# The first up projection fed row block by row block, later transfers held back, and two transposes moved into the third unit

## The reference

```python
def rmsnorm(x, g):
    y = x * lax.rsqrt(jnp.mean(x * x, axis=-1, keepdims=True) + EPS)
    return y * g

def swiglu(x, w_gate, w_up, w_down):
    return (jax.nn.silu(x @ w_gate) * (x @ w_up)) @ w_down

x = x + 0.5 * swiglu(rmsnorm(x, ffn1_norm), ffn1_w_gate, ffn1_w_up, ffn1_w_down)
# then: a mixer (gated delta rule and spatial gating), two more feed-forwards with a
# norm between them, a Mamba-2 mixer with a short convolution, cross attention,
# a fourth feed-forward and a final norm
```

## Time and profile before

| | us |
|---|---|
| time, median of 3 runs | 1371.12 (1370.67 to 1371.12) |
| the profiled execution's own time | 1371.11 |
| its span, first to last instruction | 1369.3 |
| TensorE busy | 1356.1 |
| ScalarE busy | 706.9 |
| VectorE busy | 622.0 |
| GpSimd busy | 548.8 |
| mean granted TensorE clock | 0.999 of full |

### The profile page before, as it was taken

One profiled execution on the slowest core, in us unless ns is written; L12 is line 12 of the kernel. 1 busy time (PEld: TensorE's weight loads), 2 busy tenths in 40 slices (PEclk: granted clock), 3 DMA queues, 4 the chain that ended last, 5 costly groups with the idle time before them and its releaser, 6 DMA issues.

```text
span 1369.3 us, 16611 instructions
## 1 busy us (share of the span) xinstructions
PE 1356.1 (99%) x6542; PEld 1130.5 (83%) x6542; DVE 622.0 (45%) x746; ACT 706.9 (52%) x910; POOL 548.8 (40%) x190
## 2 busy tenths in 40 slices
PE   8999999999999999999999999999999999999997
PEld 6888888998888888888888888888888888888886
DVE  4333346864333343333336559764335632433334
ACT  6444447345544445444347787657434644544432
POOL 2444443453544444444543331034535522444443
PEclk9999999999999999999999999999999999999999
DMA  9655554223555455555554555345754442655550
GB/s 362 217 184 184 185 184 154 93 90 127 200 184 184 169 176 211 197 187 189 188 192 154 217 176 193 123 154 174 289 182 169 178 176 96 217 195 184 184 184 31
DMA packets 38369, 244.21 MB, mean 178 GB/s; under 512 B 5888, under 2 KB 6304, under 8 KB 10272
## 3 DMA queue, kind: packets, MB, share of 16 engines
q1 hardware_dynamic: 35968, 234.66, 49.3%
q10 hardware_dynamic: 2336, 8.65, 1.7%
HBM read 242.21 MB, written 1.08 MB: 178 GB/s over the span
## 4 chain that ended last, share of the span: by engine, by line
PE 95%; DVE 2%; SPq 1%; ACT 1%; DMA 1%; issue 0%; POOL 0%; ACTq 0%; DVEq 0%
PE acc L329 27%; PE acc L331 27%; PE acc L330 27%; PE work L930 2%; PE acc L2468 2%; PE work L527 1%; PE work L845 1%; PE acc L2469 1%; SPq L499 1%; PE work L1752 1%; PE work L369 1%; DVE conv_out L879 1%; DMA raw<-in_t_ffn_up 1%; PE work L2492 1%; PE work L2515 1%; DVE wlo L310 0%
## 5 line engine op out<-in xcount | busy, mean ns | idle before, releaser
L310 POOL TENSOR_TENSOR wlo<-raw,whi 128x2048 fp32r<-128x2048 f32 (+1 forms) x105 | 488.2, 4653 | 642.2 <-ACT whi L305 634.3
L305 ACT ACTIVATE whi<-raw 128x2048 fp32r<-128x2048 f32 x222 | 415.8, 1884 | 93.6 <-PE acc L331 87.3
L329 PE MATMUL acc<-whi,xT 128*128 128x512 f32 x1120 | 448.0, 400 | 3.1 <-DVE xT L296 2.8
L331 PE MATMUL acc<-whi,xT 128*128 128x512 f32 x1120 | 437.8, 391 | 0.0
L330 PE MATMUL acc<-wlo,xT 128*128 128x512 f32 x1120 | 436.7, 390 | 0.0
L310 DVE TENSOR_TENSOR wlo<-raw,whi 128x2048 fp32r<-128x2048 f32 x117 | 301.6, 2578 | 239.4 <-ACT whi L305 239.2
L329 PEld LDWEIGHTS acc<-whi,xT 128*128 128x128 f32 x1120 | 210.7, 188 | 47.2 <-issue 2.7
L331 PEld LDWEIGHTS acc<-whi,xT 128*128 128x128 f32 x1120 | 210.4, 188 | 45.0
L330 PEld LDWEIGHTS acc<-wlo,xT 128*128 128x128 f32 x1120 | 211.0, 188 | 40.4 <-issue 0.2
L329 PE MATMUL acc<-whi,hid_hi 128*128 128x512 f32 x352 | 137.8, 391 | 0.0
L331 PE MATMUL acc<-whi,hid_lo 128*128 128x512 f32 x352 | 137.2, 390 | 0.0
(11 more groups left out here) (381 smaller groups left out, 1382.1 us busy)
## 6 DMA issues: line engine op xcount, KB each, us to landing
raw<-in_t_ffn_up SPq DMA_DIRECT2D x86, 1024.0 KB, 5.0
raw<-in_t_m_in SPq DMA_DIRECT2D x52, 1024.0 KB, 5.1
raw<-in_t_ffn_down SPq DMA_DIRECT2D x40, 1024.0 KB, 4.9
raw<-in_t_m_os SPq DMA_DIRECT2D x8, 1024.0 KB, 7.0
raw<-in_t_ffn_down SPq DMA_DIRECT2D x8, 512.0 KB, 3.3
raw<-in_t_m_out SPq DMA_DIRECT2D x4, 1024.0 KB, 5.1
sum_rows<-row_scratch ACTq DMA_DIRECT2D x4, 1024.0 KB, 4.7
raw<-in_t_m_oa SPq DMA_DIRECT2D x4, 1024.0 KB, 5.1
```

Of the source, the lines that this page charges most:

```text
L305: act.activation(granule(whi, u, i), granule(raw, u, i), ACT.Copy).then_inc(hi_ready, 1)
L310: eng.tensor_tensor(granule(wlo, u, i), granule(raw, u, i), granule(whi, u, i).bitcast(F32), ALU.subtract).then_inc(lo_odd if g % 2 else l ...
L329: pe.matmul(to, xhi[:, kt, tok], hi, start=first, stop=False)
L331: return pe.matmul(to, xlo[:, kt, tok], hi, start=False, stop=last)
```

## The change

- Unit 0's weights come in single row blocks for granule 0, x pieces 0 and 1 singly. ScalarE rounds one row block of weights and one x piece in turn for all eight, VectorE makes all eight low parts (GpSimd had the last two).
- TensorE orders each row block of unit 0 as two hi-hi products (both token tiles), two hi-lo, two lo-hi, with a wait of its own ahead of each pair.
- Granule 2 is transferred, rounded and made low in two halves. Granule 3's low part moves from GpSimd to VectorE.
- SyncE waits for an earlier landing before each next group of transfers; the 16 parameter transfers move behind the up units' loads.
- In the first layer the transposes of hidden chunk 0 move from the middle of unit 1 to the middle of unit 2, ahead of those of chunk 1.
- Granule 4's transfer waits for `lo_even` at 5, which is the first half of granule 2's low part (`FIRST_LO` has 4 in place of 3; granule 0 counts four).

```diff
-FIRST_HI, FIRST_LO, FIRST_XLO = 4, (3, 1), 6
+FIRST_HI, FIRST_LO, FIRST_XLO = 7, (4, 3), 6
...
     def multiply_first(pe, u, banks):
...
+            pe.wait_ge(hi_ready, kt + 1)
+            pe.wait_ge(xhi_done, kt + 1)
+            for t in range(NT):
+                pe.matmul(banks[t], xT_hi[:, kt, toks[t]], hi[:, j, :], start=kt == 0, stop=False)
+            pe.wait_ge(lo_odd if i else lo_even, j + 1)
+            for t in range(NT):
+                pe.matmul(banks[t], xT_hi[:, kt, toks[t]], lo[:, j, :], start=False, stop=False)
             pe.wait_ge(xlo_done, kt + 1)
             for t in range(NT):
-                mm = triple(pe, banks[t], xT_hi, xT_lo, kt, t, hi[:, j, :], lo[:, j, :], kt == 0, kt == KD - 1)
+                mm = pe.matmul(banks[t], xT_lo[:, kt, toks[t]], hi[:, j, :], start=False, stop=kt == KD - 1)
...
         if f == 0:
-            load_first(sp, 0, (0,), up_tiles[0], S["first_w0"])
-            load_first(sp, 0, (1,), up_tiles[0], S["first_w1"])
-            load_first(sp, 0, (2, 3), up_tiles[0], raw_ready[0])
-            load_x_first(sp, 2, (4, 8))
-            load_first(sp, 1, (0, 1), up_tiles[0], S["second_w"])
+            for kt in range(4):
+                load_first(sp, 0, (kt,), up_tiles[0], (S["first_w0"], S["first_w1"], S["third_pieces"], raw_ready[0])[kt])
+            sp.wait_ge(S["first_w0"], 16)
+            load_x_first(sp, "fifth_pieces", (4, 6))
+            load_first(sp, 1, (0, 1), up_tiles[0], S["fifth_pieces"])
+            sp.wait_ge(S["first_w1"], 16)
+            load_x_first(sp, "x_first6", (6, 8))
             load_first(sp, 1, (2, 3), up_tiles[0], raw_ready[1])
-            for i in range(2):
-                load(sp, units["ffn0.up1"], i, up_tiles[1])
+            sp.wait_ge(raw_ready[0], 16)
+            load_first(sp, 2, (0, 1), up_tiles[1], S["third_w"], 0)
+            load_first(sp, 2, (2, 3), up_tiles[1], raw_ready[2], 0)
+            sp.wait_ge(S["fifth_pieces"], 32)
+            load(sp, units["ffn0.up1"], 1, up_tiles[1])
+            sp.wait_ge(raw_ready[1], 16)
             for half in range(2):
                 load_x(sp, half)
-            for dst, src in PARAMS:
-                sp.dma_start(dst, src).then_inc(params_loaded, 16)
...
         up(10)
+        if f == 0:
+            for dst, src in PARAMS:
+                sp.dma_start(dst, src).then_inc(params_loaded, 16)
...
-        up(1, halfway=lambda: ffn_hidden_t(pe, f, 0))
-        up(2, halfway=lambda: ffn_hidden_t(pe, f, 1))
+        if f == 0:
+            up(1)
+            up(2, halfway=lambda: (ffn_hidden_t(pe, f, 0), ffn_hidden_t(pe, f, 1)))
+        else:
+            up(1, halfway=lambda: ffn_hidden_t(pe, f, 0))
+            up(2, halfway=lambda: ffn_hidden_t(pe, f, 1))
...
-        split_hi(act, units[f"ffn{f}.up1"], 0)
+        if b:
+            split_hi(act, units[f"ffn{f}.up1"], 0)
         split_hi(act, units[f"ffn{f}.up1"], 1)
...
-        step(0)
-        if f == 0:
+        if f:
+            step(0)
+        else:
+            wait_lo(pool, units["ffn0.up1"].g + 1)
             reciprocal_rms(pool, 0)
...
     def start_scalar(act):
-        act.dma_start(gain[:, :, :], w["p_gains"]).then_inc(S["gains_loaded"], 16)
-        load_x_first(act, 0, (0, 2))
-        load_x_first(act, 1, (2, 4))
+        load_x_first(act, "x_first0", (0, 1))
+        act.dma_start(gain[:, :, :], w["p_gains"]).then_inc(S["x_first0"], 16)
+        load_x_first(act, "x_first1", (1, 2))
+        load_x_first(act, "third_pieces", (2, 4))
...
+        for kt in range(KD):
+            split_hi_first(act, kt // 4, (kt % 4,), *weights[kt], hi_ready)
+            if kt in x_pieces:
+                act.wait_ge(*x_pieces[kt])
+            round_first(act, kt)
+        split_hi_first(act, 2, (0, 1), S["third_w"], 16, hi_ready)
+        split_hi_first(act, 2, (2, 3), raw_ready[2], 16, hi_ready)
 
     def start_vector(dve):
-        for kt in range(4):
-            split_lo_first(dve, 0, (kt,), (hi_ready, kt + 1), lo_even)
+        for kt in range(KD):
+            split_lo_first(dve, kt // 4, (kt % 4,), (hi_ready, kt + 1), lo_odd if kt // 4 else lo_even)
             rest_first(dve, kt)
-        split_lo_first(dve, 1, (0, 1), (hi_ready, 5), lo_odd)
-        for kt in (4, 5, 6, 7):
-            rest_first(dve, kt)
+        split_lo_first(dve, 2, (0, 1), (hi_ready, KD + 1), lo_even)
+        split_lo_first(dve, 2, (2, 3), (hi_ready, KD + 2), lo_even)
+        split_lo(dve, units["ffn0.up1"], 1)
```

More of the change, by code:

```diff
@@ L276, in first_piece, with load_first, split_hi_first @@
         return buf[:, granule, kts[0] * KT:(kts[-1] + 1) * KT]
-    def load_first(sp, granule, kts, tile, signal):
-        at = 4 * granule * KT
+    def load_first(sp, granule, kts, tile, signal, at=None):
+        at = 4 * granule * KT if at is None else at
         sp.dma_start(first_piece(raw, granule, kts), tile[:, at + kts[0] * KT:at + (kts[-1] + 1) * KT]).then_inc(signal, 16)
-    def split_hi_first(act, granule, kts, loaded, signal):
-        act.wait_ge(loaded, 16)
+    def split_hi_first(act, granule, kts, loaded, count, signal):
+        act.wait_ge(loaded, count)
         act.activation(first_piece(whi, granule, kts), first_piece(raw, granule, kts), ACT.Copy).then_inc(signal, 1)
@@ L333, in multiply_first @@
     def multiply_first(pe, u, banks):
+        toks = [slice(t * P, (t + 1) * P) for t in range(NT)]
         for kt in range(KD):
             i, j = divmod(kt, 4)
[L337 to L340, removed]
+            hi, lo = granule(whi, u, i), granule(wlo, u, i)
+            pe.wait_ge(hi_ready, kt + 1)
[5 more added lines that the diff above has]
+                pe.matmul(banks[t], xT_hi[:, kt, toks[t]], lo[:, j, :], start=False, stop=False)
             pe.wait_ge(xlo_done, kt + 1)
-            hi, lo = granule(whi, u, i), granule(wlo, u, i)
             for t in range(NT):
-                mm = triple(pe, banks[t], xT_hi, xT_lo, kt, t, hi[:, j, :], lo[:, j, :], kt == 0, kt == KD - 1)
+                mm = pe.matmul(banks[t], xT_lo[:, kt, toks[t]], hi[:, j, :], start=False, stop=kt == KD - 1)
             if j == 3:
@@ L681, in ffn_vector @@
             rest_xt(dve, b, 1)
-        split_lo(dve, units[f"ffn{f}.up1"], 0)
+            split_lo(dve, units[f"ffn{f}.up1"], 0)
         step(1)
@@ L2765, in start_scalar @@
         await_own(act)
[L2766 to L2783, removed]
+        weights = ((S["first_w0"], 16), (S["first_w1"], 16), (S["third_pieces"], 32), (raw_ready[0], 16),
+                   (S["fifth_pieces"], 32), (S["fifth_pieces"], 32), (raw_ready[1], 16), (raw_ready[1], 16))
+        x_pieces = {0: (S["x_first0"], 32), 1: (S["x_first1"], 16), 6: (S["x_first6"], 16)}
+        for kt in range(KD):
[5 more added lines that the diff above has]
+        split_hi_first(act, 2, (2, 3), raw_ready[2], 16, hi_ready)
     def start_vector(dve):
-        for kt in range(4):
-            split_lo_first(dve, 0, (kt,), (hi_ready, kt + 1), lo_even)
+        for kt in range(KD):
+            split_lo_first(dve, kt // 4, (kt % 4,), (hi_ready, kt + 1), lo_odd if kt // 4 else lo_even)
             rest_first(dve, kt)
-        split_lo_first(dve, 1, (0, 1), (hi_ready, 5), lo_odd)
-        for kt in (4, 5, 6, 7):
-            rest_first(dve, kt)
+        split_lo_first(dve, 2, (0, 1), (hi_ready, KD + 1), lo_even)
+        split_lo_first(dve, 2, (2, 3), (hi_ready, KD + 2), lo_even)
+        split_lo(dve, units["ffn0.up1"], 1)
     def start_pool(pool):
@@ L2796, in start_pool, with load_x_first @@
         pool.wait_ge(half_const, 2)
-        pool.wait_ge(lo_odd, 1)
-        split_lo_first(pool, 1, (2, 3), (hi_ready, 6), lo_odd)
-    def load_x_first(eng, part, kts):
+    def load_x_first(eng, signal, kts):
         c = slice(*kts)
-        eng.dma_start(x_first[:, c, :], w["t_x"][:, c, :]).then_inc(S[f"x_first{part}"], 16)
+        eng.dma_start(x_first[:, c, :], w["t_x"][:, c, :]).then_inc(S[signal], 16)
     def start_tensor(pe):
```

## The result

| | before | after |
|---|---|---|
| median of 6 runs, us | 1370.95 | 1376.95 |
| profiled execution, own time / span, us | 1371.11 / 1369.3 | 1377.75 / 1375.7 |
| ratio of the runs, 95% interval | | 1.0043 (1.0033 to 1.0053) |

The change makes the kernel 6.0 us slower. 1376.3 was forecast, and the profiled execution of after is the slowest of its six.

The account below looks back on a forecast made before the run. TensorE, busy almost without a break, was taken as the bound, so granule 5's lateness is the end's. Granule 4 4.25 us earlier, 7.5 lost behind: 3.3, plus 1.9 for the clock, 5.2 on 1371.1: 1376.3 us, range 1373.0 to 1378.3.

Parts of the forecast that it names:

- two dates: TensorE's starts of granule 4 (29.1, 4.25 us earlier) and granule 5 (42.5, 3.3 us later); the end is as late as granule 5.
- the step that decided: Moved transposes in unit 2: granule 5's split and low part queue behind the rounding, 7.88 us from transposes to granule 5.
- Case A: Between granules 4 and 5: stall of 3.3 us net plus clock fall of 1.9, 5.2 us slower; chance 0.5.
- the 4.2 us at the end of the kernel: Time from TensorE's last product to the clock's fall in the trace of before, used to judge whether the stall drops it.
- The front: Stretch up to granule 4: start at 29.1, 4.25 us earlier than before, bounds 27.8 and 30.2.
- case D: Front gains nothing (granule 4 at 31 to 33) or parameters cost 1 to 3 us: 7 to 9 us slower; chance 0.08.
- The other chain: TensorE's own way to granule 4: first product 5.6, four granules 22.2 us, waits 0.5 to 1.5: 28.3 to 29.3.
- C: The front's gain pays for the stall, granule 4 before 28.55, not slower by the bound; chance 0.1.
- D's second half: Parameter issues behind the up units' loads exceed one us of slack and delay the next weights, 1 to 3 us.
- B: Between granules 4 and 5: the stall, but the clock stays up, 3.3 us slower, 1374.4; chance 0.3.

Follow-up runs that it names:

- e2: The changed kernel with the transposes back where they were (chunk 0 in the middle of unit 1, chunk 1 of unit 2): 1369.47 us, ratio to before 0.9987.
- e3: The changed kernel, transposes still moved, with ScalarE's and VectorE's lists for chunks 0 and 1 reordered to suit: 1367.66 us, ratio to before 0.9974.
- e4: The kernel before with only the transposes moved: 1382.27 us, ratio to before 1.0078.
- e1: The changed kernel with 17 unread products of ones between the two pairs of moved transposes and 11 behind the second: 1374.69 us, ratio to before 1.0025.
- e8: The changed kernel with only the 17 products of ones between the two pairs of transposes: 1376.48 us, ratio to before 1.0040.
- e5: The kernel of e3 without SyncE's five waits ahead of the first two units' transfers: 1368.84 us, ratio to before 0.9985.
- e9: The changed kernel with only the 11 products of ones behind the second pair of transposes: 1376.28 us, ratio to before 1.0040.
- e10: The kernel of e3 without the last two of SyncE's five waits (ahead of granule 3 and of x): 1368.42 us, ratio to before 0.9979.
- e6: The kernel of e3 with the 16 parameter transfers back in front of the loop, behind x: 1373.94 us, ratio to before 1.0021.

## Why the prediction was right

**The place and the mechanism.** The sum rested on two dates, and the step that decided was that GpSimd's low part of granule 5 is queued behind a rounding that now waits for granule 4's products. e2, e3 and e4 show it from three sides: with the transposes back the loss is gone, with ScalarE's and VectorE's order put right it turns into a gain, and with the move alone the same 7.68 us are there. 7.88 was forecast for that piece from the rows one granule on.

**The clock.** Case A (stall and fall) came true; 1.9 us were taken, the trace shows 1.9, and e1 gives 2.3 as the difference of the medians. The chance was argued too cautiously. I set the idle time between the transposes against the 4.2 us at the end of the kernel; a wait of 2.7 (e8), of 2.9 (e4), and once of 1.8 us (e5) had a fall in it or right behind. The rule of the Trainium skill cited there (TensorE: Matmul & The Clock Gate, Part 4: transposes don't count as busy in the same way) is not decided by these runs: the fall came 0.2 us (e9) and 0.45 us (after) behind the start of the second transposes, so they did not prevent it, but the wait behind them is enough by itself (e8).

**The front, mis-sized.** Granule 4 was put at 29.1 and started at 30.82 in the profile, outside my bound of 30.2 and close to the 31 at which case D begins. The step that failed is "ScalarE ends the squares of x and starts the table load at 22.63, as before, since the same weights and x must have come". It started at 24.36, because granule 3 was there later: its rounding began at 19.25, 1.7 us later than before. The near explanation is the hold. Granule 3's transfer now waits until the fifth and sixth row blocks and their x have landed, and was issued at 12.05. But this is not shown, and e5 and e10 speak against it: issued 4.4 and 1.8 us earlier than in e3, granule 3 was there no earlier. What the traces show is a spread. In the seven kernels with all holds granule 3 was issued between 10.60 and 12.05, and its rounding began 6.95 to 7.2 us behind that. At the early end stands e8, with the same front as after: issue at 10.60, rounding at 17.60, then the table load at 22.70 and granule 4 at 29.17, both as forecast. In e3, in between, granule 4 came at 29.89; in e1 at 31.04, which also waited for granule 4's weights. Why the first pieces, on which that issue waits, land up to 1.5 us earlier in one execution than in another stays open.

The other chain was late as well. TensorE's first product came at 5.87 (5.6 was forecast), but its first pair took 1.19 us where later ones take 0.6 to 0.7, and waits of 0.56, 0.33 and 0.44 us followed. Granule 2 began at 19.39, 2.4 us later than the products alone need from 5.87, where 0.5 to 1.5 had been added. So even without the late granule 3 TensorE would have been at granule 4 at 30.5.

**What hid it.** Front 1.7 us worse than forecast, stall 0.2 better: 4.76 instead of 3.3 us at granule 5, and 6.6 with the clock instead of 5.2. The medians differ by 6.0. The hit within 0.7 us owes something to the range of the executions; the profiled one, with the late front, is 0.8 us slower than the median.

**The other cases.** C (the front pays for the stall) did not come: granule 4 would have had to start before 28.55, and the earliest of the traces has 29.17 (e8). D's second half, the parameters, did not happen: 8.3 us of issues against 15.4 at worst. The next weights were issued at 118.98; with the 5.1 us that such a transfer takes in this stretch they are there at 124.1, 7.9 us before ScalarE takes them. B is excluded by the windows.

## What to carry to other kernels

When the point at which one engine does a step is moved, read the other engines' lists from that step's consumer on: everything that is written behind the consumer moves too, needed or not. Here the four transposes of one hidden chunk (the title says two) moved by one unit delayed a weight split that had nothing to do with them, and the repair was to rewrite the order of two other lists. And a kernel in which TensorE is otherwise always busy can pay for a wait twice: once for its length, and once for the half clock behind it, as here for waits of 2.7 us and more.

## What the runs showed of the hardware

- The granted clock fell to the lower level 2.0 us into a wait of 4.28 (e6), 2.4 into one of 2.86 (e4) and 2.6 into one of 2.67 (e8). Of the waits of 3.76 us ahead of the second transposes one had the fall in it (e4, at 43.9), two had it 0.2 and 0.45 us behind them (e9, after). In one execution it came 0.9 us behind a wait of 1.82 us, with products already running (e5), while waits of 1.3 us (before) and 1.94 us (e2) passed without a fall near them. So the length of one wait does not settle it. I had expected to need about 4.
- It came back 2.9 to 5.4 us after TensorE had work again (e9: 40.50 to 43.4; e4: 34.13 to 37.1; e8: 42.40 to 45.8; after: 44.03 to 48.0; e6: 33.65 to 38.2; e4 again: 48.77 to 54.2). In e9 that work was products of ones, and it did as well as real ones.
- 28 products of ones in the stall made the kernel 2.3 us faster with no other edit.
- The same 16 parameter issues took 15.4 us right behind the first weights and x, single ones up to 2.4; in e6, behind held transfers, 7.6 us at 0.43 to 0.47 each, and behind the loop 8.3 us. That a full queue is the reason was my reading; no run isolates it.
- Granule 3's transfer (1 MB), issued 1.8 us (e10) and 4.4 us (e5) earlier than in e3, landed no earlier.
